# Memory's keys and values computed inside the last mixing turns, and the output projection by token halves

## The reference, cut to what matters

```python
x = x + 0.5 * swiglu(rmsnorm(x, ffn1_norm[l]), ...)
h = rmsnorm(x, mix_norm[l])
q, k, v, z_rwkv, gate_a, gate_b = _split(h @ w_in[l], IN_SIZES)
...
merged = jax.nn.sigmoid(gate_a) * o_a + jax.nn.sigmoid(gate_b) * o_b
x = x + merged @ w_out[l]
x = x + memory_cross_attention(rmsnorm(x, cross_norm[l]), rmsnorm(mem, mem_norm[l]),
                               w_cq[l], w_ckv[l], w_co[l])
x = x + 0.5 * swiglu(rmsnorm(x, ffn2_norm[l]), ...)

def memory_cross_attention(h, m, w_cq, w_ckv, w_co):
    q = (h @ w_cq).reshape(b, s, X_HEADS, X_HEAD_DIM)
    mk, mv = _split(m @ w_ckv, (D_MODEL, D_MODEL))
    ...
    return out @ w_co
```

## Time and profile before

| what | value |
|---|---|
| median of 3 runs | 3301.32 us (3301.2 to 3301.44) |
| profiled execution, its own time | 3303.52 us |
| its span, first to last instruction | 3301.7 us |
| PE busy | 2963.9 us (90%) |
| DVE, ACT, POOL busy | 1598.2, 1055.4, 1300.2 us |
| granted TensorE clock, mean over the span | 0.947 of full speed |

### The profile page before, as it was taken

One profiled execution on the slowest core, in us unless ns is written; L12 is line 12 of the kernel. 1 busy time (PEld: TensorE's weight loads), 2 busy tenths in 40 slices (PEclk: granted clock), 3 DMA queues, 4 the chain that ended last, 5 costly groups with the idle time before them and its releaser, 6 DMA issues. The chain is left out here.

```text
span 3301.7 us, 61575 instructions
## 1 busy us (share of the span) xinstructions
PE 2963.9 (90%) x26974; PEld 2434.4 (74%) x26974; DVE 1598.2 (48%) x1747; ACT 1055.4 (32%) x1718; POOL 1300.2 (39%) x667
## 2 busy tenths in 40 slices
PE   3899999996899999999999986797976799999995
PEld 2688888884678877787877765786755588887885
DVE  6654444444166556656655662113222744453445
ACT  2433333222234334433434432212121333333221
POOL 1344444442364545455544541222131344444441
PEclk7999999997999999999999986898988899999997
DMA  3222224433221111322111100611002222234441
GB/s 139 80 96 80 80 103 166 144 121 134 59 62 58 52 45 45 96 63 63 52 45 45 53 21 9 229 52 32 19 26 89 64 80 77 78 108 159 144 144 67
DMA packets 247432, 270.71 MB, mean 82 GB/s; under 512 B 13184, under 2 KB 204800, under 8 KB 245120
## 3 DMA queue, kind: packets, MB, share of 16 engines
q1 hardware_dynamic: 247168, 266.81, 24.6%
HBM read 218.54 MB, written 48.23 MB: 81 GB/s over the span
## 5 line engine op out<-in xcount | busy, mean ns | idle before, releaser
L459 POOL TENSOR_TENSOR w_low<-ffn_work,w_high 128x1024 fp32r<-128x1024 f32 x182 | 445.0, 2446 | 668.6 <-ACT w_high L532 393.9
L499 PE MATMUL bank<-h_high,w_high 128*128 128x512 f32 x1232 | 484.6, 393 | 57.6 <-DVE h_low L643 34.6
L499 PE MATMUL bank<-h_low,w_high 128*128 128x512 f32 x1232 | 483.3, 392 | 0.0
L499 PE MATMUL bank<-h_high,w_low 128*128 128x512 f32 x1232 | 482.9, 392 | 0.0
L1076 POOL TENSOR_TENSOR mix_panel_low<-arena,mix_panel_high 128x1024 fp32r<-128x1024 f32 x96 | 233.0, 2427 | 343.6 <-ACT mix_panel_high L1442 343.6
L1171 PE MATMUL bank<-mix_h_high,mix_panel_high 128*128 128x512 f32 x768 | 317.6, 414 | 20.0 <-POOL mix_panel_low L1076 14.9
L690 DVE TENSOR_TENSOR h_low<-ffn_work,h_high 128x512 fp32r<-128x512 f32 x88 | 205.7, 2337 | 250.7 <-ACT h_high L547 250.7
L499 PEld LDWEIGHTS bank<-h_high,w_high 128*128 128x128 f32 x1232 | 233.9, 190 | 110.9 <-issue 60.1
L1171 PE MATMUL bank<-mix_h_low,mix_panel_high 128*128 128x512 f32 x768 | 304.4, 396 | 0.0
L1171 PE MATMUL bank<-mix_h_high,mix_panel_low 128*128 128x512 f32 x768 | 303.3, 395 | 0.0
L516 PE MATMUL bank<-h_high,w_high 128*128 128x512 f32 x704 | 275.2, 391 | 4.6 <-DVE h_low L690 4.6
(11 more groups left out here) (263 smaller groups left out, 5822.8 us busy)
## 6 DMA issues: line engine op xcount, KB each, us to landing
arena<-w_in SPq DMA_DIRECT2D x96, 512.0 KB, 3.8
ffn_work<-w_down SPq DMA_DIRECT2D x88, 512.0 KB, 3.6
a_spill<-ffn_work SPq DMA_DIRECT2D x88, 256.0 KB, 2.3
ffn_work<-a_spill SPq DMA_DIRECT2D x88, 256.0 KB, 2.7
ffn_work<-w_gate SPq DMA_DIRECT2D x12, 1024.0 KB, 5.7
ffn_work<-w_up SPq DMA_DIRECT2D x12, 1024.0 KB, 8.2
arena<-x_spill SPq DMA_DIRECT2D x3, 4096.0 KB, 14.2
arena<-w_gate SPq DMA_DIRECT2D x10, 1024.0 KB, 5.6
```

The costliest lines, as they stand in the source:

```text
L459: nc.gpsimd.tensor_tensor(slot(w[1], q), src, slot(w[0], q).bitcast(F32), ALU.subtract).then_inc(s_low, 1)
L499: last = mm(bank[:, bk, :], w[wp][:, q % RING, kt, e], h[hp][:, k, kt], start=fresh and kt + wp + hp == 0, stop=kt == KT // 2 - 1 and wp = ...
```

## The change

The change has three parts.

1. **Memory is normed in `shared()`.** Its rows are loaded into the norm's two buffers once they are free, squared and scaled on ACT, transposed on PE (8 transposes behind panel 2 and 8 behind panel 3), and made into high and low parts by ACT and DVE, which are written to `mem_spill` (2 loads and 2 stores of 1 MB more). The spill of x is issued later than before.
2. **Keys and values are units of the mixer.** Panels 96 to 111 are the 16 panels of `w_ckv`, each 24 matmuls of 256 columns with fp32r parts: five in `prepare(15)`, one in fifths in `solve(15)`, five in `prepare(16)`, one in `solve(16)` with one matmul in each of the chain's 24 slots, four in `prepare(17)`. Panels 112 and 113 are the first two of `w_out`; "units" 114 to 117 are the four pairs of channel tiles of the merged output's first half, loaded, rounded and subtracted in the same two slots. The parts of memory are loaded into the space of the first token half (`hA`) when the last real panel is done.
3. **`cross()` begins with the output projection by token halves**: 16 products `k` of 24 matmuls of 512 columns, panels of `w_out` loaded twice. The norm is two norms `nx[0]` and `nx[1]` of 512 tokens each. `nx[0]` runs inside the second half's products, `nx[1]` beside the first query products (`project_first`). Ahead of the products stand 16 transposes of the memory's values.

```diff
+            mem_rows, mem_sq = nrm.sq, nrm.acc
+            mem_sum, mem_mean, mem_root = space(MT), space(MT), space(MT)
+            s_mem, s_msq, s_mmean, s_mroot = sem("mem_loaded"), sem("mem_squared"), sem("mem_averaged"), sem("mem_rooted")
...
+                    for t in range(MT):
+                        sp.dma_start(mem_rows[t], d["mem"][t * P:(t + 1) * P, :]).then_inc(s_mem, 16)
+                    sp.dma_start(x_spill[:, :], xT[:].rearrange("p a b -> p (a b)")).then_inc(s_spill, 16)
...
+                    sp.wait_ge(s_mlow, KT)
+                    for w in range(2):
+                        sp.dma_start(mem_spill[w], mem_parts[w][:].rearrange("p a b -> p (a b)").bitcast(F32)).then_inc(
+                            s_spill, 16)
+                    sp.wait_ge(s_spill, 80)
...
+                        if 2 <= j < 4:
+                            if j == 2:
+                                pe.wait_ge(s_mscaled, MT)
+                            else:
+                                pe.wait_ge(s_mlow, KT // 2)
+                            for kt in range(4 * (j - 2), 4 * (j - 1)):
+                                for t in range(MT):
+                                    last = nc.tensor.transpose(mem_bank(kt)[:, t * P:(t + 1) * P],
+                                                               mem_rows[t][:, kt * P:(kt + 1) * P], c("ident"))
+                            last.then_inc(s_mtr, 1)
...
+                        elif j == 1:
+                            act.wait_ge(s_mroot, 1)
+                            for t in range(MT):
+                                nc.scalar.activation(mem_rows[t], mem_rows[t], ACT.Copy,
+                                                     scale=mem_root[:, t:t + 1]).then_inc(s_mscaled, 1)
+                        elif j < 4:
+                            act.wait_ge(s_mtr, j - 1)
+                            for kt in range(4 * (j - 2), 4 * (j - 1)):
+                                nc.scalar.activation(mem_parts[0][:, kt], mem_bank(kt), ACT.Copy,
+                                                     scale=gain("mem_norm", kt)).then_inc(s_mhigh, 1)
...
+            KV, OUT, SRC = UNITS, UNITS + 2 * KT, UNITS + 2 * KT + 2
+            ALL = SRC + KT // 2
+            mem_in = [hA[w][:, 0:KT // 2].rearrange("p a b -> p (a b)").rearrange("p (a b) -> p a b", b=NMEM)
+                      for w in range(2)]
+
+            def points(i):
+
+                if i <= ITER:
+                    return [NP * (i + 1) + j for j in range(NP - 1)]
+                return list(range(NP * (ITER + 1) + NP, OUT))
+
+            def inside(i):
+
+                return [NP * (i + 2) - 1]
...
+                        if unit < KV:
+                            src = w_in[:, :, col(unit):col(unit) + P]
+                        elif unit < OUT:
+                            src = wkv[:, :, (unit - KV) * P:(unit - KV + 1) * P]
+                        elif unit < SRC:
+                            src = w_out[:, :, (unit - OUT) * P:(unit - OUT + 1) * P]
+                        else:
+                            if unit == SRC:
+                                for j in range(2):
+                                    sp.wait_ge(s_mw[j], 16 * (PAIRS // 2))
+                            k = 2 * (unit - SRC)
+                            src = m_spill.rearrange("p (k t) -> p k t", t=T)[:, k:k + 2, 0:HALF]
+                            dst = raw[unit % 2].rearrange("p a b -> p (a b)").rearrange("p (a b) -> p a b", b=HALF)
+                        sp.dma_start(dst, src).then_inc(s_raw[unit % 2], 16)
...
+                    def load_mem():
+                        sp.wait_ge(S("proj_ready"), UNITS)
+                        for w in range(2):
+                            sp.dma_start(mem_in[w].rearrange("p a b -> p (a b)").bitcast(F32), mem_spill[w]).then_inc(
+                                s_memin, 16)
...
+                        low, high, src = pw[1][:, unit % 2], pw[0][:, unit % 2], raw[unit % 2]
+                        if unit >= SRC:
+                            k = 2 * (unit - SRC)
+                            low, high = hA[1][:, k:k + 2], hA[0][:, k:k + 2]
+                            src = src.rearrange("p a b -> p (a b)").rearrange("p (a b) -> p a b", b=HALF)
+                        G.tensor_tensor(low, src, high.bitcast(F32), ALU.subtract).then_inc(S("panel_low"), 1)
...
+                            if unit >= KV:
+                                dst, src = bank[:, unit % 2, 0:NMEM], mem_in[hp][:, kt]
+                            last = mm(dst, pw[wp][:, unit % 2, kt], src, start=term == 0, stop=term == TERMS - 1)
...
-                                project(NP * (i + 2) - 1, n * TERMS // 5, (n + 1) * TERMS // 5)
+                                project(inside(i)[0], n * TERMS // 5, (n + 1) * TERMS // 5)
+                            elif not live and s >= FIRST_CHAIN:
+                                project(inside(i)[0], s - FIRST_CHAIN, s - FIRST_CHAIN + 1)
...
+                        if unit >= 2:
+                            act.wait_ge(S("proj_ready"), min(unit - 1, OUT))
+                        high, src = pw[0][:, unit % 2], raw[unit % 2]
+                        if unit >= SRC:
+                            k = 2 * (unit - SRC)
+                            high = hA[0][:, k:k + 2]
+                            src = src.rearrange("p a b -> p (a b)").rearrange("p (a b) -> p a b", b=HALF)
...
+                        if i <= ITER:
+                            store(inside(i)[-1])
+                            round_panel(inside(i)[-1] + 2)
+                    for unit in range(SRC, ALL):
+                        round_panel(unit)
...
+            nx = [Norm(xT[:, :, n * HALF:(n + 1) * HALF], rn, "cross_norm", HALF, parts=[[src[0][n]], [src[1][n]]], bk=7)
+                  for n in range(2)]
...
+                    for k in range(Q):
+                        n, o = divmod(k, KT)
+                        panel_ready(pe, k)
+                        if k < 4:
+                            pe.wait_ge(s_vst, k % 4 + 1)
+                        else:
+                            pe.wait_ge(s_padd, k - 3)
+                        for kt in range(KT):
+                            if k == KT:
+                                pe.wait_ge(s_slow, kt + 1)
+                            for wp, hp in THREE:
+                                last = mm(bank[:, k % 4, :], pw[wp][:, k % 2, kt], src[hp][n][:, kt],
+                                          start=kt + wp + hp == 0, stop=kt == KT - 1 and wp == 1)
+                        last.then_inc(s_ready, 1)
+                        if k == KT:
+                            nx[0].pe_sums(pe)
+                        elif k == KT + 1:
+                            nx[0].pe_scale(pe)
...
+                    for k in range(2, KT + 2):
+                        subtract_low(pool, k % 2, k)
+                        if k >= 4:
+                            subtract_source(pool, 1, k - 4, k - 3)
+                    for kt in range(KT - 2, KT):
+                        subtract_source(pool, 1, kt, kt + 1)
+                    nx[0].pool_root(pool)
+                    for k in range(KT + 2, KT + 4):
+                        subtract_low(pool, k % 2, k)
+                    nx[0].pool_low(pool)
+                    for k in range(KT + 4, Q + 2):
...
+                    for k in range(2, KT + 2):
+                        round_high(act, k % 2, k, k // 2)
+                        if k >= 4:
+                            if (k - 4) % 4 == 0:
+                                act.wait_ge(s_merged[(k - 4) // 4], 16)
+                            round_source(act, 1, k - 4)
+                        if k > 2:
+                            act.wait_ge(s_padd, k - 2)
+                            nx[0].square(act, k - 3)
+                    for kt in range(KT - 2, KT):
+                        round_source(act, 1, kt)
+                    act.wait_ge(s_padd, KT)
+                    nx[0].square(act, KT - 1)
+                    for k in range(KT + 2, Q + 2):
+                        round_high(act, k % 2, k, k // 2)
+                        if k == KT + 3:
+                            nx[0].act_high(act)
+                        if k > KT + 2:
+                            act.wait_ge(s_padd, k - 2)
+                            nx[1].square(act, k - KT - 3)
+                    act.wait_ge(s_padd, Q)
+                    nx[1].square(act, KT - 1)
 
...
+                    def project_first():
+                        nx[0].wait(pe, KT - 2)
+                        nx[0].wait(pe, KT - 1)
+                        panel_ready(pe, Q)
+                        terms(0, 0, 0, KT // 2)
+                        nx[1].pe_sums(pe)
+                        terms(0, 0, KT // 2, KT)
+                        panel_ready(pe, Q + 1)
+                        terms(1, 0, 0, KT // 2)
+                        nx[1].pe_scale(pe)
+                        terms(1, 0, KT // 2, KT)
```

(6 more changed lines are left out.)

496 lines of the change are left out of this document (251 added, 245 removed).

## The result

The changed kernel takes 3281.77 us in the median (3278.68 to 3286.37, 4 runs) where the kernel before takes 3301.26 (3301.18 to 3301.44): a ratio of 0.9942, with 95% interval 0.9925 to 0.9959. That is 19.5 us less. The forecast was 3256.4 (44.9 less) with a range of 3243 to 3276, so the sign was right and the size was not, and the time lies outside the range. The profiled execution took 3284.51, its span is 3282.7.

The account below looks back on a forecast made before the run. PE was taken to bound full turns and the output projection, DVE or step latency the last turn and chain. Seven stage terms sum to -44.9: 3303.5 profiled becomes 3258.6, and the median, 2.2 lower, 3256.4; range 3243 to 3276.

Parts of the forecast that it names:

- Unit price: Keys and values in the mixer: one unit of 24 matmuls of 256 columns takes 2.8 us of PE, at most 5.44.
- case of loads in line: Rival, chance 0.10: weight loads are not hidden beside matmuls, a unit takes 5.4 us instead of 2.8, total 3281.
- Turn 15: Mixer turn that gets six units: 55.2 to 66.4 us, +11.2, with DVE slowed by POOL's subtractions.
- `prepare(16)`: Mixer stage before the last chain: five units at POOL's pace of 3.6 us take it from 10.3 to 19, +8.7.
- PE doesn't need these before the chain: In `prepare(16)`: DVE's copy, gate and merge of the "out" part were taken as not needed by PE before the chain.
- Last chain: Chain with one unit matmul in each slot: 23.7 to 22 us, -1.7, between bounds of 18.5 and 25.5.
- halfway value: Last chain: 22 us, taken between 25.5 if the clock stays low and 18.5 if it holds at 1.00.
- Chain's end: From the last chain's end to the first output product: 101.8 to 41.3 us, -60.5, bounds 31 and 52.
- Output projection: Output projection by token halves: 87.3 to 99.3 us, +12.0, same columns but added waits, bounds 3 and 20.
- Added waits: Output projection: waits at product 8 (2.9) and product 12 (5.8), with sums and scale 1.6 and low-clock start 1.5: 11.8 us.
- Norm: Norm and first query product: 47.7 to 31.1 us, -16.6, half-products cover the second norm's root, bounds 25 and 47.7.
- `shared()`: Memory's norm ahead of the mixer: +2.0 us, its transposes on PE, the other work beside five panels.

Follow-up runs that it names:

- entry_dummies: The changed kernel plus 20 products of 512 columns that nobody reads, ahead of the last chain: median 3276.11 us, ratio 0.9922 to the kernel before.

## Why the forecast was off, step by step

- **Unit price (2.8): right.** A unit's matmuls of 256 columns start 0.12 us apart:

```profile
2020.44 0.38 PE L1307 MATMUL bank<-mix_h_high,mix_panel_high 128*128 128x256 f32 x1
2020.66 0.28 PE L1307 MATMUL bank<-mix_h_low,mix_panel_high 128*128 128x256 f32 x1
2020.78 0.28 PE L1307 MATMUL bank<-mix_h_high,mix_panel_low 128*128 128x256 f32 x1
```

  The case of loads in line gives 0.22 and is refuted, although its time (3281) is the one that was measured. The Trainium skill, "TensorE: Matmul & The Clock Gate", section "The mechanism", would have a weight load overlap only matmuls of another row group; these matmuls use all rows, and the trace doesn't agree with it. The same section also lets a load into a background weight buffer be pulled ahead, and with that the trace agrees.
- **Turn 15 (+11.2; measured +11.1): right**, and for the reason given, DVE behind POOL's subtractions. That DVE hides the reload held to within 2 us.
- **`prepare(16)` (+8.7; +10.6): near in size, with one wrong reading.** "PE doesn't need these before the chain" is not so: ahead of the chain stands `pe.wait_ge(S("merged_ready"), i - 1)`, and PE waits 2.40 for DVE's last step of the "out" part (L1836) in the changed kernel's profile, 4.59 in five others. Without this wait the stage has 18.5, the forecast's 19. The sign that was named, waits for POOL's low parts, isn't there in this profile.
- **Last chain (-1.7; +6.5): the step that failed** is "one of them (0.23) stands before a step that DVE waits for: 3.2 a chunk, 25.5" as the upper bound, and the halfway value. At the low clock, which the chain had before too, all three matmuls of a chunk are on the path, at 0.27 each: 3.8 a chunk, 30.2 in all. At the upper clock the chain takes 20.4 (entry_dummies). A filled entry gave the second; halfway came in no profile. The wait ahead of the chain, which the forecast left out, was what the sum had to look at; why the clock falls behind some short waits there and not behind others stays open.
- **Chain's end (-60.5; -59.2): right**, and term by term: the four units take 15.1 (13.6), the last piece's subtraction ends at +33.7 (+32.1), PE stands until +39.3 (37.4), and the transposes take 3.3 (3.8).
- **Output projection (+12.0; +24.1): the main step that failed.** "Added waits" priced each at its own length, and only "first products at a low clock after the idle" (1.5) had a second price. The waits at products 8 and 12 came as worked out (2.9, 5.94 for 5.8), but 13 and 14 matmuls at 0.43 followed them. And product 4's wait of 3.99, with 11 such matmuls, was left out: the change puts 4 MB in front of a panel's load in one queue, and the sum priced no transfer there.
- **Norm (-16.6; -13.2):** the chain of pairs was right; the wait at the block's end has the same second price, about 2, and is 0.8 longer than the 3.8 taken.
- **`shared()` (+2.0):** the mixer's first load is issued 2.3 us later (857.94 for 855.67), but `solve(14)` begins only 0.2 later; where 2 us are given back wasn't followed.

The sign came out right since the largest term (-60.5) held. The range was too narrow since its cases moved one term at a time, while the low clock hit three terms together.

## What to carry to other kernels

Price every wait of PE that a change adds twice: its length, and the matmuls behind it at half pace (here 0.2 us for each of 7 to 14 of 512 columns, so 1.5 to 3 us, behind waits of 3 to 6). Where a serial stretch with little work follows, the second price can be the whole stretch, so let the last movable work of PE stand in the wait ahead of it. A program that moves a stage must have its loads looked at in issue order: what is wanted first must not stand behind a bulk reload.
